# The first RMSNorm of a macaron block: sums of squares taken from the token rows as they arrive

## The reference

```
h += 1/2 SwiGLU(RMSNorm(h)) ;  h += StickBreakingAttention(RMSNorm(h)) ;  h += 1/2 SwiGLU(RMSNorm(h))
out = RMSNorm(h), meta tokens dropped
rmsnorm(x, gain) = x * rsqrt(mean(x*x, axis=-1) + 1e-5) * gain
swiglu(u) = (silu(u @ w_gate) * (u @ w_up)) @ w_out      # 1024 -> 2816 -> 1024, float32
```

## Time and profile before

| | |
|---|---|
| median of 3 runs | 1979.63 us |
| the profiled execution's own time | 1981.68 us |
| its span (first to last instruction) | 1979.8 us |
| granted TensorE clock, mean | 0.993 |
| PE busy | 1912.8 us (97%) |
| DVE, ACT, POOL busy | 1309.2 (66%), 750.0 (38%), 1091.7 (55%) |
| first plain product begins | 34.73 us |

### The profile page before, as it was taken

One profiled execution on the slowest core, in us unless ns is written; L12 is line 12 of the kernel. 1 busy time (PEld: TensorE's weight loads), 2 busy tenths in 40 slices (PEclk: granted clock), 3 DMA queues, 4 the chain that ended last, 5 costly groups with the idle time before them and its releaser, 6 DMA issues. The chain is left out here.

```text
span 1979.8 us, 37528 instructions
## 1 busy us (share of the span) xinstructions
PE 1912.8 (97%) x12572; PEld 1748.1 (88%) x12572; DVE 1309.2 (66%) x1737; ACT 750.0 (38%) x1495; POOL 1091.7 (55%) x1010
## 2 busy tenths in 40 slices
PE   7899999999999999999999999999999999989998
PEld 6899999999999989999989987778887888768877
DVE  5867777776666768333379981297777777666674
ACT  5433343333222235222267762253333343322232
POOL 4456665655555645445477762346666666555561
PEclk9999999999999999999999999999999999999999
DMA  4234434355877411323332112013444444587742
GB/s 129 75 119 142 163 124 159 118 170 194 303 246 246 153 44 54 114 94 108 101 100 84 64 54 64 22 32 128 148 145 162 133 142 152 181 325 242 247 149 96
DMA packets 244613, 273.59 MB, mean 138 GB/s; under 512 B 12976, under 2 KB 176816, under 8 KB 244544
## 3 DMA queue, kind: packets, MB, share of 16 engines
q1 hardware_dynamic: 244544, 272.69, 41.8%
HBM read 179.58 MB, written 93.06 MB: 138 GB/s over the span
## 5 line engine op out<-in xcount | busy, mean ns | idle before, releaser
L1806 PE MATMUL psum<-arena 128*128 128x260 f32 (+3 forms) x3908 | 1246.1, 319 | 47.6 <-DVE scratch L1545 8.5
L1808 PE MATMUL psum<-arena 128*128 128x260 f32 (+3 forms) x3908 | 1229.0, 314 | 0.0
L1807 PE MATMUL psum<-arena 128*128 128x260 f32 (+3 forms) x3908 | 1226.4, 314 | 0.0
L1806 PEld LDWEIGHTS psum<-arena 128*128 128x128 f32 x3908 | 739.9, 189 | 106.4 <-issue 16.6
L1807 PEld LDWEIGHTS psum<-arena 128*128 128x128 f32 x3908 | 738.8, 189 | 45.6 <-issue 3.4
L1808 PEld LDWEIGHTS psum<-arena 128*128 128x128 f32 x3908 | 739.1, 189 | 43.8
L702 POOL TENSOR_TENSOR arena<-scratch,arena 128x512 fp32r<-128x512 f32 x365 | 518.7, 1447 | 409.3 <-ACT arena L950 409.3
L1398 DVE TENSOR_TENSOR scratch<-scratch,psum 128x520 f32<-128x520 f32 (+1 forms) x265 | 182.8, 690 | 243.6 <-PE psum L1808 180.2
L950 ACT ACTIVATE arena<-scratch 128x512 fp32r<-128x512 f32 x371 | 214.5, 622 | 321.6 <-DVE scratch L1401 119.3
L1401 DVE TENSOR_TENSOR scratch<-scratch 128x512 f32<-128x512 f32 x200 | 253.8, 1269 | 110.3 <-POOL arena L702 103.9
L794 POOL TENSOR_TENSOR arena<-scratch,arena 128x256 fp32r<-128x256 f32 x280 | 212.8, 780 | 183.0 <-ACT arena L1161 183.0
(11 more groups left out here) (94 smaller groups left out, 1298.6 us busy)
## 6 DMA issues: line engine op xcount, KB each, us to landing
scratch<-w_in_dram SPq DMA_DIRECT2D x88, 512.0 KB, 4.9
pairs<-scratch SPq DMA_DIRECT2D x140, 260.0 KB, 4.1
arena<-pairs SPq DMA_DIRECT2D x35, 1040.0 KB, 9.0
pairs<-scratch SPq DMA_DIRECT2D x140, 256.0 KB, 3.9
arena<-pairs SPq DMA_DIRECT2D x35, 1024.0 KB, 9.4
scratch<-w_out_dram SPq DMA_DIRECT2D x80, 256.0 KB, 3.1
qkv<-scratch SPq DMA_DIRECT2D x48, 260.0 KB, 2.1
scratch<-w_qkv_dram SPq DMA_DIRECT2D x24, 512.0 KB, 4.8
```

The lines of the kernel that those rows point to most:

```text
L1806: nc.tensor.matmul(dst, wh, xh, start=start, stop=False, skip_group_check=True)
L1807: nc.tensor.matmul(dst, wh, xl, start=False, stop=False, skip_group_check=True)
L1808: return nc.tensor.matmul(dst, wl, xh, start=False, stop=stop, skip_group_check=True)
```

## The change

The sums of squares are no longer taken from the transposed `h` by ones-matmuls, but from the rows in `x_tiles` (tokens on partitions) by ACT's Square with an accumulated sum, one instruction of 1024 columns per tile, as soon as the tile lands. Root and reciprocal work on 5 and on 4 columns. PE then writes each token's reciprocal to all partitions in PSUM (`spread`): six matmuls per half, with the column of reciprocals repeated 128 times as weights and pieces of the identity as moving data. The first half's spread stands behind tile 5's transposes, the second half's behind the first plain product.

Moved with it:
- SP loads the plain weights ahead of tiles 5 to 8.
- DVE copies all eight k-tiles of tiles 5 to 8 (two copies a tile); ACT copies only tiles 0 to 4. The four rows of B11 stand between the copies of tiles 5 to 8, ahead of the second half's reciprocal.
- ACT's high halves of B11 stand between the squares of tiles 7 and 8 and around the second root; `early_weights` moves behind the high halves of B12.
- POOL makes the low halves of B12 ahead of those of weights 0 and 4.
- PE's first plain product waits for the last copy of tile 8.

```diff
+def low_copies(t):
+    return t + 1 if t in X_TILES[0] else 2 * t - X_TILES[0][-1] + 1
...
+        x_rstd = stats[:].rearrange("p a b -> p (a b)")
+        x_squares = piece(scratch, 3072, 2, D_MODEL)
...
-            for t in range(1, META_TILE + 1):
+            for t in X_TILES[0][1:]:
                 load_x(t)
-
             load_plain(FFN1)
+            for t in X_TILES[1]:
+                load_x(t)
...
+                if n == FFN1:
+                    rows_lo(n, 7)
                 weight_lo(n, 0, 1)
                 weight_lo(n, 4, 2)
                 if n != FFN1:
                     rows_lo(n, 0)
                     rows_lo(n, 4)
-                rows_lo(n, 7)
+                    rows_lo(n, 7)
...
+            def square_x(t):
+                n = tile_rows(t)
+                act.wait_ge(landed[t], 16)
+                wait(act, squared, t - 1)
+                nc.scalar.activation(x_squares[0:n, t % 2], x_tiles[0:n, t], ACT.Square, accum_out=x_rstd[0:n, t:t + 1])\
+                    .then_inc(squared, 1)
+            def root_x(c):
+                cols = x_rstd[:, X_TILES[c][0]:X_TILES[c][-1] + 1]
+                act.wait_ge(squared, X_TILES[c][-1] + 1)
+                nc.scalar.activation(cols, cols, ACT.Sqrt, scale=1.0 / D_MODEL, bias=eps[:, 0:1])\
+                    .then_inc(root_taken, 1)
+            def norm_first():
+                nc.scalar.preload_act_table(ACT.Sqrt)
+                square_x(0)
+                for t in X_TILES[0][1:]:
+                    take_high(t - 1)
+                    square_x(t)
+                root_x(0)
+                take_high(X_TILES[0][-1])
+                plain_weights(FFN1)
+                for t in X_TILES[1]:
+                    square_x(t)
+                    if t >= X_TILES[1][2]:
+                        split_rows(FFN1, 0, (t - X_TILES[1][2],))
+                root_x(1)
+                split_rows(FFN1, 0, (2, 3))
+                split_rows(FFN1, 4)
...
                 def first_unit():
                     split_rows(n, 7)
+                    if n == FFN1:
+                        early_weights(n)
                     plain_gate(0)
...
+            def take_low(t):
+                cols = tile_rows(t)
                 dve.wait_ge(x_transposed, t + 1)
+                for high in range(1 if t in X_TILES[0] else 2):
+                    src = psum[:, 2 * (t % 2) + high, :].rearrange("p (k c) -> p k c", k=4)[:, :, 0:cols]
+                    nc.vector.tensor_copy(h[:, 4 * high:4 * high + 4, t * P:t * P + cols], src).then_inc(h_low, 1)
...
+            for t in X_TILES[0]:
+                take_low(t)
+            reciprocal_x(0)
             dve.wait_ge(gains_loaded, 16)
-            dve.wait_ge(h_low, META_TILE + 1)
-            reciprocal(FFN1, 0)
-            rows(FFN1, "B11")
+            for k, t in enumerate(X_TILES[1]):
+                take_low(t)
+                rows(FFN1, "B11", (k,))
+            reciprocal_x(1)
             rows(FFN1, "B21")
-            reciprocal(FFN1, 1)
             rows_lo(FFN1, 4)
...
+            def spread(c):
+                pe.wait_ge(rstd, c + 1)
+                cols = HALF[FFN1] // 2
+                for j in range(2):
+                    begin = c * HALF[FFN1] + j * cols
+                    for t in range(begin // P, (begin + cols - 1) // P + 1):
+                        rows, at, end = tile_rows(t), max(begin, t * P), min(begin + cols, t * P + tile_rows(t))
+                        last = nc.tensor.matmul(psum[:, NORM_BANKS[FFN1][c] + j, at - begin:end - begin],
+                                                x_rstd[0:rows, t:t + 1].to_broadcast([rows, P]),
+                                                ident[0:rows, at - t * P:end - t * P], start=True, stop=True)
+                last.then_inc(summed, 1)
...
+                    else:
+                        pe.wait_ge(h_low, low_copies(META_TILE))
...
+                        if n == FFN1 and i == 0:
+                            spread(1)
...
-            for c in range(len(X_TILES)):
-                transpose_x(c)
-                sums(0, c)
+            for t in range(X_TILES[1][1]):
+                transpose_x(t)
+            spread(0)
+            for t in range(X_TILES[1][1], META_TILE + 1):
+                transpose_x(t)
```

More of the change, by code:

```diff
@@ L102, with tile_rows, squares_to, sums_to @@
 X_TILES = [range(0, 5), range(5, META_TILE + 1)]
+X_SQUARES, X_SPREADS = META_TILE + 1, 2
+def tile_rows(t):
+    return META if t == META_TILE else P
+def squares_to(n):
+    return X_SQUARES + 2 * KT * (n - 1)
+def sums_to(n):
+    return X_SPREADS + 2 * KT * (n - 1)
+def low_copies(t):
+    return t + 1 if t in X_TILES[0] else 2 * t - X_TILES[0][-1] + 1
 TILES = META_TILE + 1
@@ L1177, in down @@
                 nc.scalar.activation(wd[n][:, 0], raw_d, ACT.Copy).then_inc(s["d_hi"], 1)
[L1179 to L1180 removed]
+            act.wait_ge(zero_set, 3)
+            norm_first()
             units(FFN1)
@@ L1319, in reciprocal, with rows @@
                 nc.vector.reciprocal(sums, sums).then_inc(rstd, 1)
-            def rows(n, name):
+            def rows(n, name, ks=range(HK)):
                 (kt, c), half = ROWS[name], HALF[n]
-                dve.wait_ge(rstd, 2 * n + c + 1)
-                for k in range(HK):
+                if n == FFN1:
+                    dve.wait_ge(summed, c + 1)
+                    dve.wait_ge(h_low, low_copies(X_TILES[c][-1]))
+                    dve.wait_ge(h_high, X_TILES[0][-1] + 1)
+                else:
+                    dve.wait_ge(rstd, 2 * n + c + 1)
+                for k in ks:
                     nc.vector.scalar_tensor_tensor(out=part(n, name, k),
@@ L1808, in product, with transpose_x @@
                 return nc.tensor.matmul(dst, wl, xh, start=False, stop=stop, skip_group_check=True)
-            def transpose_x(c):
-                for t in X_TILES[c]:
-                    rows = META if t == META_TILE else P
-                    pe.wait_ge(landed[t], 16)
-                    if t >= 2:
-                        pe.wait_ge(h_low, t - 1)
-                        pe.wait_ge(h_high, t - 1)
-                    for kt in range(KT):
-                        dst = psum[:, 2 * (t % 2) + kt // 4, (kt % 4) * P:(kt % 4) * P + rows]
-                        last = nc.tensor.transpose(dst, x_tiles[0:rows, t, kt * P:(kt + 1) * P],
-                                                   ident[0:rows, 0:rows])
-                    last.then_inc(x_transposed, 1)
+            def transpose_x(t):
+                rows = tile_rows(t)
+                pe.wait_ge(landed[t], 16)
+                if t >= 2:
+                    pe.wait_ge(h_low, low_copies(t - 2))
+                    pe.wait_ge(h_high, min(t - 1, X_TILES[0][-1] + 1))
+                for kt in range(KT):
+                    dst = psum[:, 2 * (t % 2) + kt // 4, (kt % 4) * P:(kt % 4) * P + rows]
+                    last = nc.tensor.transpose(dst, x_tiles[0:rows, t, kt * P:(kt + 1) * P], ident[0:rows, 0:rows])
+                last.then_inc(x_transposed, 1)
+            def spread(c):
[9 more added lines that the diff above has]
+                last.then_inc(summed, 1)
             def sums(n, c, ats=range(KT)):
```

42 lines of the change are left out of this document (16 added, 26 removed).

## The result

The changed kernel took 1966.7 us (4 runs, 1965.96 to 1967.81), the kernel before 1980.95 beside it (4 runs): ratio 0.9927, interval 0.9915 to 0.9940. With all later repeats of both kernels it is 1967.5 on average over 19 runs (1963.97 to 1972.19) against 1981.0 over 76 (1976.75 to 1986.57): 13.6 us less, ratio 0.9931 (0.9926 to 0.9937).

The account below looks back on a forecast made before the run. Before 90 us DVE's queue, not PE's, was taken as the path. Its final lead, 10.5 or 8.5 us, middle 9.5, less 0.8 for PE's clock, gave 8.7 off 1979.63: 1970.9 us, range 1967.2 to 1976.

Parts of the forecast that it names:

- the low case: Second half of the front with PE at 1.2 GHz: B21 complete at 29.4, DVE's lead there 9.2 us.
- Collision with the mixes: DVE's low halves of B21 meeting POOL's three mixes: 5.7 us against 6.5 before, 0.8 gained when they meet fully.
- DVE's wait for ACT: Before B22's low halves, behind ACT's early weights and plain gate: DVE waits 1.5 us instead of 0.49.
- plain product 4: PE's product that waits for B22: 37.8 or 39.9 us against 50.69, so 12.9 or 10.8 earlier.
- the 1.11 that DVE no longer waits: DVE's wait at 67.04 goes; a last POOL operation may take back half: lead 10.5 or 8.5 us.
- the two cases: PE's clock at 2.4 or 1.2 GHz from tile 5 on: final DVE lead of 10.5 or 8.5 us.
- the Sum: Final step: middle of 10.5 and 8.5, 9.5, less 0.8, gives 8.7 us gained and a time of 1970.9.
- PE's clock: Clock falls again after PE's longer wait, perhaps already at v1: 0.8 us more lost than before, bounds -1.6 and +3.
- A: Rival: DVE gives nothing back and PE's lead at its fifth plain product passes whole: 12.9 us, 1966.7; 10%.
- B: Rival: front later, x5 to x7 landing 2 to 3 us later or low clock lasting: gain 5 to 6, 1974; 17%.
- C: Rival: at the unit loop the second unit's weights or their low halves come no earlier: 1978; 6%.
- D: Rival: PE stays at 1.2 GHz through the plain and first unit: 21 us later, 2001; 4%.

Follow-up runs that it names:

- spread_early: The changed kernel with the second spread ahead of the first plain product instead of behind it; 1968.62 us, ratio 0.9934 to the kernel before.
- b_same: The kernel before, unchanged, profiled a second time; 1980.68 us, ratio 1.0007.
- a_again: The changed kernel, unchanged, profiled and timed once more; 1967.5 us, ratio 0.9928 to the kernel before.
- warm: The changed kernel with 18 identity matmuls that nothing reads between the transposes of tiles 4 and 5; 1969.23 us, ratio 0.9942 to the kernel before.
- b_shift: The kernel before with 18 unread identity matmuls of 8 columns, 9 ahead of each of two blocks of transposes in the front; 1980.19 us, ratio 0.9992.
- pad20: The changed kernel with 20 unread identity matmuls, 10 ahead of tile 5's transposes and 10 behind tile 8's; 1968.9 us, ratio 0.9935 to the kernel before.

## Why the prediction missed

The mechanism of the front was right. DVE's queue is its path, and most steps came out where they were put:

- Squares 1.04 us apart instead of 1.2; they cost DVE nothing. The spread took 2.55 at the low clock and 1.40 at the high one (1.3 and twice that).
- x5 landed at 16.11 (15.6). The clock was the low case after all, half way: B21's low halves at 28.5, between 26.7 and 29.5; first plain product 25.2 (24).
- Collision with the mixes 5.54 (5.7; three at 1.65 and one at 0.63 are 5.6); DVE's wait for ACT 1.52 (1.5); B22's low halves at 40.87 (39.4 to 41.4), 4.45 long (4.9; with all four behind a POOL operation it would have been 6.6). Lead at T1 8.8 to 9.5 (7.9 to 9.9). PE's wait for "w" ended at 73.11 (71 to 73).
- Wrong without a price: PE did not wait at plain product 4, which it began at 40.3 (38 to 40), and waited 2.43 before v1, not 3.4.
- Wrong with a small price: the 1.11 that DVE no longer waits was to come back by half. T3's low halves took 3.61 us instead of 2.53, which takes back all of it: the lead at the low halves of T2 and T4 is 9.2 on average, where the two cases have 9.5.

**The failed step is the Sum**, in two of its terms.

First, PE's clock, taken at 0.8 us of loss, was a gain of 0.9. I had the place nearly right ("perhaps already at v1", and it began at 67.8, 1 us into v1) but priced the fall at 0.8 more than the old one. It cost 0.6: DVE waited 0.55 for PE ahead of "w", and the wait before v5, 1.62 instead of spread_early's 2.50, took up the rest. The old fall at 82.5 lay on the product that the last addition waited for, with no wait of PE's behind it, and its going was worth 1.5, as b_same shows within one kernel. So the front gave 9.2 on average at the low halves of T2 and T4 (9.5 was forecast), 8.3 to 8.9 at "w", and 1.5 behind it: 9.8 to 10.5, not 8.7. The Trainium skill (TensorE: Matmul & The Clock Gate, "What's actually happening") sees the fall as the price of an idle array; the trace agrees that each fall of the changed kernel's front followed a wait (of 2.28, 2.11 and 2.43 us), and adds that its price depends on the waits that follow: 0.6 at 67.8, 1.5 at 82.5, for the same 3.4 us.

Second, the sum had no term behind 90 us, since PE is full there. It is not full everywhere. Behind the front the changed kernel won another 3.5 us on average (the 13.6 of all times, less the 10.1 of its four leads). 1.3 to 1.9 of them came at the attention's start, where a fall of the clock did not come again once the instruction fetch had moved off the 8 KB load. A view of the waits beyond the front would have shown the 2.0 us there and the fall behind it; that 40 records fewer would move them, I could not have told without the experiments.

What stays open is where the other 2 come from. They wander between executions, most of all at the way down (484 to 497), where the DMA engines are at 99 to 101%: there the lead changes by -0.2 to 2.2. The fall of the clock at 495.5 in the kernel before does not pay for it: PE in the changed kernel gains 1.5 over these 3.4 us and gives 1.7 back by 504. PE's wait there was 3.5 and 3.2 in the kernel before and 1.5, 1.0, 3.3 and 2.2 in the changed one:

```profile
495.64 0.58 PE L1806 MATMUL psum<-arena 128*128 128x260 f32 x1 [3.48 <-DVE scratch L1545]
```
```profile
483.84 0.38 PE L1877 MATMUL psum<-arena 128*128 128x260 f32 x1 [1.54 <-DVE scratch L1612]
```
```profile
485.90 0.38 PE L1877 MATMUL psum<-arena 128*128 128x260 f32 x1 [3.32 <-DVE scratch L1612]
```

The last is the changed kernel too (a_again), so the change does not set it; what does, no run tells apart.

As to the rivals: A gave the number (1966.7) by luck, for a reason that did not happen, since DVE gave back 1.3 us between B21 and T1 as forecast. B, C and D did not come.

## What to carry to other kernels

Price a fall of the clock by the waits behind it. Here 3.4 us at half clock cost 0.6 where a wait of PE's of 2.5 us stood behind (67.8), and 1.5 to 1.6 where none was near (82.5 and 1004), and an edit that moves the last wait moves this price too. An edit of an engine's program moves its later instruction fetches; where a small load stands at the head of a chain (here 8 KB, behind which ACT, DVE and PE wait in turn), compare its landing, and the granted clock behind it, in both traces before a gain or a loss far from the edit is put down to the edit's idea. And a queue that is shortened beyond the next chain gives nothing: with a lead of 14 at B21, bought by loading the plain weights last, their chain left 8.5 at T1.

## What the runs showed of the hardware

- An instruction fetch within 1.2 us behind an 8 KB load's issue made it land at 4.5 to 5.0 instead of 3.3 to 3.7 us. At 2.8 us behind (warm) it did nothing: 3.3. This is no fixed price: for loads of the same line in the other rounds, 965 to 1125 us, a fetch within 0.5 us came with landings of 3.25 to 4.37 us in twelve cases (4.37 in warm at 968.6, 4.15 in the kernel before at 979.9, 3.64 in b_same at 978.7), and 127 loads with none within 1.3 us took 2.9 to 3.7.
- A 128-column f32 matmul that is not a transpose stands as two records, 0.23 us for both (36 in 4.18), a transpose as one. With 8 columns in place of 128 a pair still took 0.23 (b_shift: 18 records in 2.07) and, where the clock fell in between, 0.28 (36 in 5.07): the width was not what cost.
- The granted clock fell at different places in executions of one kernel: 7 to 9 stretches in the four of the changed kernel, 5 to 9 in all 18, most of them 3.4 us long; those at 1313 to 1332, 1719 to 1735 and at the end are in all. Four profiled executions of the changed kernel ended 5.9 us apart; the longest is the one with nine.
- When DVE's low halves and POOL's mixes met, it was not always DVE that paid. In the changed kernel POOL began 0.3 ahead, and the four low halves took 5.54; in pad20 DVE began 0.9 ahead, and they took 2.52 and POOL's three mixes 5.54 (4.66 in the changed kernel):

```profile
26.56 2.52 DVE L1415 TENSOR_TENSOR arena<-plain,arena 128x520 fp32r<-128x520 f32 x4
```
```profile
27.46 5.54 POOL L755 TENSOR_TENSOR scratch<-scratch 128x512 f32<-128x512 f32 x3 [1.16 <-DMA scratch<-w_in_dram]
```
